# Router logits of a mixture-of-experts layer from 32-column weight tiles with the tokens moving

## The reference

```python
gl = (hf @ w_group) + b_group                                # 1024 x 4
el = jnp.einsum('nd,dge->nge', hf, w_erouter) + b_erouter    # 1024 x 16
```

## Time and profile before

| what | us |
|---|---|
| median of 3 runs | 1674.61 (1674.50 to 1674.83) |
| the profiled execution | 1661.31 |
| its span | 1659.6 |
| TensorE busy in the span | 1420.4 |
| VectorE busy | 1337.5 |
| ScalarE busy | 801.8 |
| POOL busy | 563.8 |

### The profile page before, as it was taken

The page is one execution under the profiler, slowest core; times in us unless marked ns, Lnnn a source line. Parts: engine busy times, 40 slices in busy tenths (PEclk is TensorE's granted clock), DMA queues, the critical chain, the costliest instruction groups (busy, mean ns, idle before and its releaser), DMA issues. The chain is left out here.

```text
span 1659.6 us, 26049 instructions
## 1 busy us (share of the span) xinstructions
PE 1420.4 (86%) x7082; PEld 786.1 (47%) x7082; DVE 1337.5 (81%) x3369; ACT 801.8 (48%) x1429; POOL 563.8 (34%) x422
## 2 busy tenths in 40 slices
PE   5977899999999999999997416999999999985573
PEld 1114555665666566665665214454455554532221
DVE  0522999989899898989997146999999999966877
ACT  0411334444444444344443102888888888862222
POOL 0002025445555443444433520212122122106775
PEclk9998899999999999999997655999999999996777
DMA  9954002111111111111011165578993323317774
GB/s 324 394 214 161 14 2 77 52 53 51 51 51 51 39 38 39 51 39 51 38 44 39 38 243 194 178 265 288 354 369 110 117 101 115 113 77 223 232 233 140
DMA packets 90721, 218.28 MB, mean 132 GB/s; under 512 B 8035, under 2 KB 42759, under 8 KB 88592
## 3 DMA queue, kind: packets, MB, share of 16 engines
q1 hardware_dynamic: 65554, 136.25, 23.5%
q0 software_dynamic: 11808, 43.00, 8.1%
q10 hardware_dynamic: 13277, 38.20, 5.9%
HBM read 165.90 MB, written 51.56 MB: 131 GB/s over the span
## 5 line engine op out<-in xcount | busy, mean ns | idle before, releaser
L968 DVE SCALAR_TENSOR_TENSOR y_sum<-uT,w_dw_cols,y_sum 128x128 f32<-128x128 f32 (+1 forms) x1972 | 511.4, 345 | 0.0
L1670 DVE SCALAR_TENSOR_TENSOR w_gate_up_lo<-w_gate_up_ring,w_gate_up_hi 128x2048 f16<-128x2048 f16 x96 | 219.3, 2286 | 23.7 <-ACT w_gate_up_hi L1595 23.5
L1595 ACT ACTIVATE w_gate_up_hi<-w_gate_up_ring 128x2048 f16 x96 | 182.8, 1906 | 60.0 <-SPq L1553 40.1
L1095 PE MATMUL bank<-w_in_hi,hT_hi 128*128 128x512 f16 (+3 forms) x544 | 194.0, 357 | 1.1 <-DVE hT_lo L1077 1.1
L1095 PE MATMUL bank<-w_in_lo,hT_hi 128*128 128x512 f16 (+3 forms) x544 | 193.6, 356 | 0.0
L1095 PE MATMUL bank<-w_in_hi,hT_lo 128*128 128x512 f16 (+3 forms) x544 | 193.6, 356 | 0.0
L1576 POOL COPY slot_index<-slot_token 128x1 int32 (+1 forms) x48 | 45.6, 950 | 351.8 <-PE eturn L1734 308.6
L1713 PE MATMUL ps_up<-w_gate_up_hi,slot_rowsT_hi 128*128 128x512 f16 x384 | 147.0, 383 | 18.2 <-DVE slot_rowsT_lo L1695 17.5
L1713 PE MATMUL ps_up<-w_gate_up_lo,slot_rowsT_hi 128*128 128x512 f16 x384 | 146.6, 382 | 0.0
L1713 PE MATMUL ps_up<-w_gate_up_hi,slot_rowsT_lo 128*128 128x512 f16 x384 | 146.5, 382 | 0.0
L726 POOL TENSOR_TENSOR y_small<-y_small,mhalf 128x1 f32<-128x1 f32 (+1 forms) x17 | 9.3, 549 | 359.7 <-DVE y_small L999 359.7
(11 more groups left out here) (252 smaller groups left out, 3015.9 us busy)
## 6 DMA issues: line engine op xcount, KB each, us to landing
w_ada_ring<-in_w_ada SPq DMA_DIRECT2D x12, 2048.0 KB, 14.9
expert_rows<-out_rows ACTq DMA_DIRECT2D x48, 512.0 KB
w_gate_up_ring<-in_w_gate SPq DMA_DIRECT2D x16, 1024.0 KB
w_gate_up_ring<-in_w_up SPq DMA_DIRECT2D x16, 1024.0 KB
w_down_ring<-in_w_down SPq DMA_DIRECT2D x16, 1024.0 KB
x_h<-in_x_prompt SPq DMA_DIRECT2D x16, 512.0 KB
x_res<-in_x_prompt SPq DMA_DIRECT2D x16, 512.0 KB, 3.4
hidden<-h SPq DMA_DIRECT2D x16, 512.0 KB, 2.6
```

Of the source, the lines that this page charges most:

```text
L968: dve.scalar_tensor_tensor(total, u, w, y_sum[:, c, :n], ALU.mult, ALU.add).then_inc(taps_done, 1)
L1095: mm = pe.matmul(out, x[xp][:, k, :n], w[wp][:, k, cols], start=(k == 0 and wp == xp), stop=(k == KD - 1 and xp == 1))
L1595: act.activation(gate_up_parts[0][:, at, k:k + KD // 2, :, :].rearrange("p k a n -> p (k a n)"), w_gate_up[:, bass.ds(b, 1), k:k + KD // 2 ...
L1670: dve.scalar_tensor_tensor(flat[1], w_gate_up[:, bass.ds(b, 1), k, :, :].rearrange("p b k a n -> p (b k a n)"), W_SCALE, flat[0], ALU.mult ...
```

## The change

The router's stationary operand becomes the weights, padded with zeros from 20 to 32 columns, and the tokens move. Product k writes partitions 32b to 32b + 31 with b = k mod 4, so that each quarter of the partitions holds the sum of two products (k = b and k = b + 4), logits down the partitions and tokens along the columns. ScalarE copies these four partial sums to SBUF (`part_logits`). One more product, with `part_logits` stationary and a constant 128x20 matrix `regroup` moving (four unit matrices below each other), adds the four quarters and turns the result back to tokens down the partitions, at columns 256 to 275 of the same bank. It stands behind the last values of the step, and `logits_done` now comes from it. In the setup POOL clears the padding and ScalarE copies `regroup` out of the unit matrix.

```diff
--- before.py
+++ after.py
@@ -165,7 +165,8 @@
             M = {
                 "w_in": [held(f"w_in_{part}", [P, KD, INW], F16) for part in ("hi", "lo")],
                 "w_out": [held(f"w_out_{part}", [P, KD, D], F16) for part in ("hi", "lo")],
-                "w_router": held("w_router", [P, KD, NR]),
+                "w_router": held("w_router", [P, KD, 32]),
+                "regroup": held("regroup", [P, NR]),
                 "bias": held("bias", [P, HEADS, 2 * P]),
                 "sink": held("sink", [P, HEADS]),
                 "nsink": held("nsink", [P, HEADS]),
@@ -253,6 +254,7 @@
         lo_ready = sem("weights_lo_ready")
         ident_ready = sem("ident_ready")
         zeroed = sem("zeroed")
+        regrouped = sem("regrouped")
         pack_turned = sem("pack_turned")
         cols_ready = sem("cols_ready")
         tanh_ready = sem("tanh_ready")
@@ -308,6 +310,7 @@
 
             @block.gpsimd
             def _(pool):
+                pool.memset(M["w_router"][:, :, NR:32], 0.0).then_inc(zeroed, 1)
                 pool.memset(K["ident"][:], 0.0).then_inc(ident_ready, 1)
                 pool.wait_ge(ident_ready, 1)
                 pool.affine_select(out=K["ident"][:], in_=K["ident"][:], compare_op=ALU.not_equal, fill=1.0,
@@ -316,7 +319,7 @@
                 pool.memset(K["mhalf"][:], -0.5).then_inc(zeroed, 1)
 
                 pool.memset(M["uT"][:, 1, :, 0:HIST], 0.0).then_inc(zeroed, 1)
-                pool.wait_ge(zeroed, 3)
+                pool.wait_ge(zeroed, 4)
 
                 pool.wait_ge(bias_turned, 1)
                 pool.memset(M["bias"][0:CHUNK, :, WIN + CHUNK:2 * P], NEG).then_inc(bias_masked, 1)
@@ -343,6 +346,9 @@
                 for i in range(RAW_RING):
                     load_piece(i)
 
+                act.wait_ge(ident_ready, 2)
+                for b in range(4):
+                    act.copy(M["regroup"][32 * b:32 * b + 32, :], K["ident"][32 * b:32 * b + 32, 32 * b:32 * b + NR]).then_inc(regrouped, 1)
                 act.wait_ge(pack_turned, 1)
                 act.copy(M["cols"][:, 0:PACKED], ps_t[:, 0, 0:PACKED]).then_inc(cols_ready, 1)
                 act.wait_ge(cols_ready, 1)
@@ -375,6 +381,7 @@
                 act.wait_ge(vec_turned, 1)
                 act.copy(vec_row[:], ps_v[0:96, :]).then_inc(vec_row_ready, 1)
                 act.wait_ge(history_ready, 2)
+                act.wait_ge(regrouped, 4)
                 act.wait_ge(dw_ready, 1)
                 act.wait_ge(small_loaded, 16 * 9)
                 act.dma_start(a["k_sample"][0:WIN - SMP], a["cache_attn_k"].rearrange("l b t h d -> (l b t) (h d)")[SMP:WIN]).then_inc(weights_loaded, 16)
@@ -528,6 +535,7 @@
         n1 = sb("n1", [P, D])
         h2 = sb("h2", [P, D])
         h2T = sb("h2T", [P, KD, P])
+        part_logits = sb("part_logits", [P, P])
         nmax = sb("nmax", [P, HEADS])
         den = sb("den", [P, HEADS])
         rden = sb("rden", [P, HEADS])
@@ -568,6 +576,8 @@
         out_done = sem("out_done")
         h2_turned = sem("h2_turned")
         logits_done = sem("logits_done")
+        parts_done = sem("router_parts_done")
+        parts_copied = sem("router_parts_copied")
 
         carried = sem("carried")
         hT_hi_ready = sem("hT_hi_ready")
@@ -885,6 +895,8 @@
                             if h == 0 and not is_tile(j, 0):
                                 act.wait_ge(logits_done, count(1, j))
                             act.copy(h2T[:, 4 * h:4 * h + 4, :n], turn_bank("h2", h)[:, :, :n]).then_inc(h2T_ready, 1)
+                        act.wait_ge(parts_done, count(1, j, 1))
+                        act.copy(part_logits[:, :n], OB["lg"][:, :n]).then_inc(parts_copied, 1)
                     if (j := lagged(i, 1)) is not None:
                         n = rows_of(j)
                         halves = halves_of(j)
@@ -1060,7 +1072,7 @@
                         j, n = j3, rows_of(j3)
                         dve.wait_ge(logits_done, count(1, j, 1))
                         t = slice(j[1], j[1] + 1) if isinstance(j[0], int) else bass.ds(j[0] * 2 + j[1], 1)
-                        dve.tensor_tensor(K["logits"][:n, t, :].rearrange("p a b -> p (a b)"), OB["lg"][:n, 0:NR], M["b_router"][:n, :],
+                        dve.tensor_tensor(K["logits"][:n, t, :].rearrange("p a b -> p (a b)"), OB["lg"][:n, 256:256 + NR], M["b_router"][:n, :],
                                           ALU.add).then_inc(logits_saved, 1)
                     if j1 is not None:
                         taps(j1, TAP_CUTS[5], TAP_CUTS[6])
@@ -1168,9 +1180,11 @@
                             pe.wait_ge(kv_ready, count(1, j0, 1))
                         else:
                             pe.wait_ge(out_copied, count(2, j3, 1))
-                        for k in range(KD):
-                            mm = pe.matmul(OB["lg"][:n, 0:NR], h2T[:, k, :n], M["w_router"][:, k, :], start=(k == 0), stop=(k == KD - 1))
-                        mm.then_inc(logits_done, 1)
+                        for half in range(2):
+                            for b in range(4):
+                                k = 4 * half + b
+                                mm = pe.matmul(OB["lg"][32 * b:32 * b + 32, 0:n], M["w_router"][:, k, :], h2T[:, k, :n], start=(half == 0), stop=(half == 1))
+                        mm.then_inc(parts_done, 1)
                     if j1 is not None:
                         j, p, n = j1, j1[1] % 2, rows_of(j1)
                         halves = halves_of(j)
@@ -1199,6 +1213,10 @@
                             if f >= 1:
                                 values(f - 1)
                         values(3)
+                    if j3 is not None:
+                        n = rows_of(j3)
+                        pe.wait_ge(parts_copied, count(1, j3, 1))
+                        pe.matmul(OB["lg"][:n, 256:256 + NR], part_logits[:, :n], M["regroup"][:], start=True, stop=True).then_inc(logits_done, 1)
                     if j0 is not None:
                         n = rows_of(j0)
                         pe.wait_ge(u_ready, count(1, j0, 1))
```

## The result

The changed kernel takes 1688.1 us (median of 4 executions, 1684.6 to 1689.1). The kernel before varies from execution to execution: in that session from 1662 to 1676 us in the runs that each kernel is compared with, and to 1682 us in e1, so that the 1674.6 us of the table ahead lie in the upper half and the profiled execution of 1661.3 us at the lower end. The profiled executions, 1687.4 and 1661.3 us, are 26 us apart.

The account below looks back on a forecast made before the run. Both TensorE and VectorE were taken as near their limit, TensorE pacing short steps, VectorE part of long ones. 37.5 (wait left) + 3 (clock) - 1.5 (last steps) + 0.4 (setup) = 39.4 us slower, 1714 us; range 1699 to 1742.

Parts of the forecast that it names:

- What bounds the kernel: Mixer steps: TensorE sets the pace in the short step, VectorE in part of the long one; any wait may show.
- The router products: TensorE's router block: four narrow tiles at once take 0.84 us in place of 1.71, a saving of 0.85 a step.
- s: TensorE's saving per step on the router products, taken as 0.85 us.
- Rival (a): Router products: the tiles run one after another, s = -0.47, 65.8 us slower in all, 1740 us; chance 0.25.
- The copy of the parts: ScalarE's copy between the h2T and pT copies: costs nothing, at most 0.2 us.
- The wait at the logits: VectorE's logits addition waits for TensorE's join: 3.2 us first, then 13 x 4.4, less 14 s; 60.4 - 14 s.
- What is swallowed: VectorE's later waits on hT_hi and uT, 11.0 us, vanish; the loop return's 13.3 us don't; 37.5 us left.
- rival (c): VectorE's loop return is swallowed too, its queue fetching during the logits wait: 13.3 us less, 1701 us; chance 0.06.
- The clock: TensorE idles 4.1 us before y_tok transposes; its clock falls once in each of 5 long steps, 3 us in all.
- Ends: Last three steps: saving 3.6 against costs 5.1, -1.5 us by its sum; setup copies on ScalarE add 0.4 us.
- The scale: Whole time: the median's 13.3 us above the profiled execution carries over, so 39.4 us is added to 1674.61.

Follow-up runs that it names:

- e1: The kernel before, unchanged, run again: median 1668.3 us, ratio 1.000.
- e4: The changed kernel with VectorE's router bias addition moved behind the last 20 taps, ahead of hT_lo: 1657.9 us, 0.994 of the kernel before.
- e6: The kernel before with its old router product moved behind the last values, no narrow tiles, copy or join: 1699.0 us, 1.018 of the kernel before.
- e8: The changed kernel with the joining product between the second and third of four rounds of values: 1661.6 us, 0.997 of the kernel before.
- e5: As e3, but all eight router products go into one 32-column tile, copy and join taking those partitions alone: 1666.2 us, 0.999 of the kernel before.
- e3: The changed kernel with the joining product ahead of the first values instead of behind the last: 1648.8 us, 0.988 of the kernel before.
- e2: The changed kernel, unchanged, run again beside the kernel before: 1686.6 us, ratio 1.010.

## Why the prediction was right in kind and wrong in size

**What bounds the kernel: right.** A wait on VectorE in front of the taps lengthens the step; e4, e6 and e8 show it from three sides.

**The router products: right, sized low.** The forecast took the end with four tiles at once, s = 0.85 us; it is 1.03 (e5 shows the other end). Going into the narrow form costs 0.1 us, and what going out costs is inside the 0.58 us; the forecast had 0.15 twice, and 0.136 us a pass where e5 has 0.11. The rule quoted from the Trainium skill ("TensorE: Matmul & The Clock Gate", Part 3), three tiles at 2.38 times the speed, gave 0.79; the four tiles here are 1.87 / 0.58 = 3.2 times as fast as one. Rival (a) is out.

**The copy of the parts: right.** It fits between the router and the first pT copy. ScalarE, start, us, line:

```profile
639.99 0.27 ACT L899 COPY part_logits<-bank 128x128 f32<-128x128 f32 x1 [5.01 <-PE bank L1186]
640.55 1.07 ACT L914 COPY pT<-turn 128x512 f32<-128x512 f32 x2 [0.29 <-PE turn L1100]
```

**The wait at the logits: right.** 60.4 - 14 s is 46.0 us with the measured s; 44.5 us were measured in 14 waits, 48.5 forecast.

**What is swallowed: the step that failed.** The forecast let 11.0 us of VectorE's old idle time vanish and kept the rest as lost. In the stage 19.3 us vanished. First, the 10.2 us on hT_hi, as forecast; the 0.8 us on uT vanished too, but stood at 860.1 us, behind the stage. Second, 6.3 us of the loop's return, which the forecast ruled out because taps and hT_lo lie between the wait and the branch (rival (c), given 0.06, is half true: the sequencer doesn't wait for the taps to end). Third, 2.8 us inside hT_lo itself. That last one was in plain sight in the earlier trace rows: the two halves of hT_lo take 1.53 us from first start to last end before and 1.28 after, because the second half started 0.24 us late, waiting for its own hT_hi, in each of 12 steps; only 0.14 us of each is idle time, too short for the list of waits. With 42.1 us of waits after the first, 42.1 - 19.3 = 22.8 us; the stage grew by 23.1.

**The clock: counted too high.** TensorE stands idle for 2.4 to 2.5 us ahead of its y_tok transposes in all five long steps, not 4.1 (0.7 to 0.9 us in the others, where the forecast had 1 to 2), and the granted clock fell from 1.00 to 0.50 (the 1.2 GHz level) behind three of them. The transposes, and the stretches behind two of them (us, PE, PEld, DVE, ACT, POOL, PEclk, DMA share, GB/s):

```profile
385.82 0.66 PE L1100 MATMUL turn<-ident,y_tok 128*128 128x128 f32 x4 [2.49 <-ACT y_tok L820]
480.24 0.66 PE L1100 MATMUL turn<-ident,y_tok 128*128 128x128 f32 x4 [2.46 <-ACT y_tok L820]
```
```profile
386.60:389.90 3.30, 3.30 (x17) 2.32 (x16) 3.04 (x9) 2.05 (x5) 1.93 (x2) 0.50 0.10 15
...
480.30:490.00 9.70, 9.70 (x60) 6.55 (x61) 9.30 (x35) 6.58 (x17) 5.57 (x5) 1.00 0.15 55
```

A long step with such a fall is 0.3 us longer than one without (48.2 us in the three, 47.9 in the two, logits to logits), since the wait for POOL behind it takes up most of it, as the forecast had said. One microsecond in all, not three, and it sits inside the waits already counted.

**Ends: not to be told from the scatter.** The first router comes 3.5 us later, where 2.8 were due (0.4 for the setup and 3.2 - s), and the last three steps are 1.1 us shorter (1.5 forecast). But e1, the kernel before once more, has 3.1 and 2.2 us more there than the profile that the forecast was read from, and e3, which doesn't wait at its first logits, comes to them 3.9 us later. What the trace does show is the last step: with the narrow product VectorE waits 10.92 us for its logits in place of 12.44, a gain of 1.5 us where the forecast had 1.7 - 1.3 = 0.4, and nothing of it comes out, as the first instruction of the routing waits for a constant from POOL, that much longer. Before and after:

```profile
970.85 0.07 DVE L1385 MEMSET equal_before<- 128x17 f32 x1 [2.97 <-POOL token_id L1338]
```
```profile
997.93 0.07 DVE L1403 MEMSET equal_before<- 128x17 f32 x1 [4.50 <-POOL token_id L1356]
```

**The scale: a miss of its own.** Adding to 1674.6 us put the forecast some 6 us too high, as the median of 18 executions in the session of e1 is 1668.5 us. Three runs within 0.4 us of each other said nothing of the scatter between executions, but the profiled execution, 13 us below them, did, and the forecast carried that difference over without asking where it came from.

So of 39.4 us forecast, 18 us came. For the stage the forecast's terms make 13 x 3.55 - 11.0 + 3 = 38.2 us, and 23 were measured: 8 of the difference are idle time of VectorE that the forecast thought lost for good, 4 the shorter waits (2 to 3 of them the larger saving), 3 the clock, whose cost is inside the waits. The other 6 us lie outside the stage, where the forecast had 1.2 us more and the medians make it 5 us less. They stay unexplained; the interval of the ratio, 1.007 to 1.013, is 12 to 21 us, so that the 23 to 25 us of the stage lie beyond it.

## What to carry to other kernels

A result belongs in a producer's queue where its consumer will ask for it: the shape of the product gained 1.0 us a step and the place of its result cost 2.7 (609.9 - 574.4 us in 13 steps), and the remedy was to move one instruction, not to undo the change. Before pricing a wait, list all idle time of the waiting engine that lies behind it, with the small gaps inside merged rows (compare first start to last end with the same row elsewhere) and the time at loop returns: here a late engine gave 19.3 of 42.1 us back from them. And ask how far whole executions lie apart before adding a difference to a median; a stretch inside the trace, here the same to 0.1 us in two profiles of the kernel before and to 2.1 us in two of the changed one, carries a comparison better.

## What the runs showed of the hardware

- Four 32-column tiles of TensorE work on fp32 products at once: 16 passes with 128 moving columns take 0.58 us in four tiles and 1.87 us in one, and the order in which the program names the tiles made no difference (0.59 us tile by tile).
- A loop's return costs VectorE 2.8 to 3.1 us from its branch to the sequencer's next instruction, whatever stood before, and 0.6 to 0.7 us with a hint of the branch; what of it shows as idle depends on how early the sequencer gets past the last wait of the round (2.7 us before, 1.4 after, 0.4 with the hint).
- Idle times of TensorE of 2.4 to 2.5 us at a granted clock of 1.00 (the 2.4 GHz level) were followed by a fall to 0.50 (1.2 GHz) in three of five cases of the changed kernel, and those of 1.1 us in none. Length alone doesn't decide it: in e2 a time of 2.51 us was followed by a fall and one of 2.63 us by none.
